# A fused two-block transformer: forget sums packed into spare rows of the first mixer's maps

## The reference, cut to what matters

```python
def forgetting_attention(q, k, v, f_logit):      # 4 heads of 64, 256 tokens
    log_f = jax.nn.log_sigmoid(f_logit)
    c = jnp.cumsum(log_f, axis=1).transpose(0, 2, 1)
    ...
        logits = jnp.einsum("bhqd,bhkd->bhqk", qi, k32) * scale
        logits = logits + ci[..., None] - c[:, :, None, :]
        logits = jnp.where(mask, logits, -jnp.inf)
        probs = jax.nn.softmax(logits, axis=-1)
        return jnp.einsum("bhqk,bhkd->bhqd", probs, v)

def multiscale_pool(v, w_pool, scale):           # 4 groups, causal windows 2, 4, 8, 16
    ...
        mean = (csum - lag) / jnp.minimum(count, w)
        outs.append(mean - g)
```

## Time and profile before

| | before |
|---|---|
| median of the runs | 971.42 us |
| lowest and highest run | 971.24 and 971.78 us |
| span of the profiled execution, first to last instruction | 969.5 us |
| PE busy | 951.9 us (98%) |
| DVE busy | 697.7 us (72%) |
| ACT busy | 521.5 us (54%) |
| POOL busy | 85.5 us (9%) |
| granted TensorE clock, mean over the span | 0.998 |

### The profile page before, as it was taken

The page is one execution under the profiler, slowest core; times in us unless marked ns, Lnnn a source line. Parts: engine busy times, 40 slices in busy tenths (PEclk is TensorE's granted clock), DMA queues, the critical chain, the costliest instruction groups (busy, mean ns, idle before and its releaser), DMA issues.

```text
span 969.5 us, 13640 instructions
## 1 busy us (share of the span) xinstructions
PE 951.9 (98%) x5566; PEld 833.2 (86%) x5566; DVE 697.7 (72%) x922; ACT 521.5 (54%) x707; POOL 85.5 (9%) x110
## 2 busy tenths in 40 slices
PE   9999999999999999999999999999999999999997
PEld 8998888888888798789988888888988798888885
DVE  5889866666658977877676666667989777666663
ACT  5888564444446556865444434368555454443432
POOL 2541100000011100000000000000132110000000
PEclk9999999999999999999999999999999999999999
DMA  9922566556645454145655565557322446756531
GB/s 302 318 94 98 191 222 217 174 182 205 198 153 196 129 165 171 47 131 174 217 174 188 186 192 178 168 172 216 114 88 75 143 143 213 224 184 193 181 122 44
DMA packets 106190, 164.40 MB, mean 170 GB/s; under 512 B 2816, under 2 KB 82784, under 8 KB 106000
## 3 DMA queue, kind: packets, MB, share of 16 engines
q1 hardware_dynamic: 104688, 158.25, 50.8%
q0 software_dynamic: 1440, 5.28, 1.5%
HBM read 162.47 MB, written 1.05 MB: 169 GB/s over the span
## 4 chain that ended last, share of the span: by engine, by line
PE 80%; DVE 12%; ACT 4%; issue 2%; POOL 1%; DMA 0%; SPq 0%; DVEq 0%; ACTq 0%
PE ps L379 78%; DVE wl L1770 3%; PE ps L387 2%; ACT xhl L1195 1%; ACT junk L1177 1%; POOL st L2559 1%; DVE st L2192 1%; DVE xf L1791 1%; DVE xhl L1787 1%; DVE rows L2395 1%; DVE h L1844 1%; DVE hs L1802 1%; DMA prm<-in_prm 0%; ACT SC L1515 0%; DVE hs L2406 0%
## 5 line engine op out<-in xcount | busy, mean ns | idle before, releaser
L1770 DVE TENSOR_TENSOR wl<-raw,wh 128x2048 fp32r<-128x2048 f32 (+2 forms) x146 | 329.8, 2262 | 142.0 <-ACT wh L1189 141.8
L1189 ACT ACTIVATE wh<-raw 128x2048 fp32r<-128x2048 f32 (+2 forms) x150 | 281.8, 1884 | 151.7 <-PE ps L379 144.1
L379 PE MATMUL ps<-xhl,wh 128*128 128x512 f32 (+1 forms) x1248 | 254.7, 350 | 0.3 <-ACT wh L1254 0.3
L379 PEld LDWEIGHTS ps<-xhl,wh 128*128 128x128 f32 x1248 | 199.3, 190 | 27.8 <-issue 1.1
L379 PE MATMUL ps<-wh,xhl 128*128 128x512 f32 (+3 forms) x1000 | 195.5, 339 | 1.6 <-issue 0.9
L379 PEld LDWEIGHTS ps<-wh,xhl 128*128 128x128 f32 x1000 | 155.3, 190 | 20.4 <-issue 1.3
L379 PEld LDWEIGHTS ps<-xhl,wl 128*128 128x128 f32 x1008 | 135.7, 191 | 7.5
L379 PE MATMUL ps<-xhl,wl 128*128 128x256 f32 x1008 | 140.6, 282 | 0.0
L379 PE MATMUL ps<-wl,xhl 128*128 128x512 f32 (+3 forms) x500 | 105.4, 336 | 1.0 <-DVE wl L1770 0.9
L379 PE MATMUL ps<-wh,fh 128*128 128x512 f32 x304 | 91.3, 392 | 1.0 <-DVE fl L2034 0.7
L379 PE MATMUL ps<-wh,fl 128*128 128x512 f32 x304 | 90.4, 390 | 0.0
(11 more groups left out here) (274 smaller groups left out, 840.0 us busy)
## 6 DMA issues: line engine op xcount, KB each, us to landing
raw<-in_ffn_gate SPq DMA_DIRECT2D x22, 1024.0 KB, 5.5
raw<-in_ffn_up SPq DMA_DIRECT2D x22, 1024.0 KB, 5.5
raw<-in_ffn_down SPq DMA_DIRECT2D x22, 1024.0 KB, 4.9
raw<-in_w_up SPq DMA_DIRECT2D x16, 1024.0 KB, 5.6
raw<-in_w_down SPq DMA_DIRECT2D x16, 1024.0 KB, 5.0
raw<-in_s_w_in SPq DMA_DIRECT2D x14, 1024.0 KB, 5.4
raw<-in_w_in SPq DMA_DIRECT2D x9, 1024.0 KB, 9.5
raw<-in_a_w_in SPq DMA_DIRECT2D x6, 1024.0 KB, 5.3
```

The lines of the kernel that those rows point to most:

```text
L379: return e.matmul(o, a, b, start=start, stop=stop, skip_group_check=True)
L1189: e.activation(high_of(i), raw_of(i), ACT.Copy).then_inc(*up("act_high", i))
L1770: e.tensor_tensor(low_of(i), raw_of(i), high_of(i).bitcast(F32), ALU.subtract).then_inc(*up("dve_lo", i))
```

## The change

Three edits, all in the first mixer.

1. The forget logits come from split weights. `wf` is now a compact tile of 8 by 4 columns with one DMA. Two tiles `wfr[0]` and `wfr[1]` of 8 by 128 columns in fp32r are cleared by POOL and then filled at columns 0 to 3 of each group of 32: ACT writes the high part (after the masks), DVE the low part (after the low part of slot 4). PE multiplies them by `xh`, `xl` and `xh`, 24 fp32r matmuls in the place of 8 fp32 ones, and the logits now lie on all four groups of 32 partitions. The softplus runs on 128 partitions.
2. The forget sums ride in the maps' queries and keys. A head has 64 query rows out of 128, the rest were zeros. DVE now writes the sums and ones there (`forget_queries`, `forget_keys`, with 0, 1 and -1 from the table `prm`), and the second fp32 product of each map is gone. `kT` of two tiles becomes `kx` of four, so ACT copies the keys in two instructions. Four memsets of POOL go.
3. The band's second block of tokens covers only the later 128 of the 256 columns.

```diff
-        NCt = sc(256)
-        CQ = sc(256)
-        rk = sc(3, 256)
+        qm = sc(4, 256)
+        kx = sc(4, 256)
+        wfr = [nc.alloc_sbuf_tensor_at(f"wf{i}", [128, 8, 128], F32R, offset=at_s + 4 * (9088 + 1024 * i)) for i in range(2)]
+        wfz = [x[:, :, :].rearrange("p k (g n) -> p k g n", g=4)[:, :, :, 0:4] for x in wfr]
+        wfg = wf.unsqueeze(2).to_broadcast([128, 8, 4, 4])
...
                     mm(o[:, lo:lo + n], q_[:, c], k_[:, 0:n], True, False)
-                    if extra:
-                        mm(o[:, lo:lo + n], extra[0][:, c], extra[1][:, 0:n], False, False)
                     d = mm(o[:, lo + n - 128:lo + n], idb[:, :], mab[:, :], False, True)
...
-                e.wait_ge(*at("dma_wf", 1))
-                for k in range(8):
-                    d = mm(ps[6][0:36, 0:256], wf[:, k, :], xf[:, k, :], k == 0, k == 7)
+                for n, (w, x) in enumerate(((wfr[0], xh), (wfr[0], xl), (wfr[1], xh))):
+                    if n == 0:
+                        e.wait_ge(*at("act_forget_high"))
+                    elif n == 2:
+                        e.wait_ge(*at("dve_forget_low"))
+                    for k in range(8):
+                        d = mm(ps[6][:, 0:256], w[:, k, :], x[:, k, :],
+                               n == 0 and k == 0, n == 2 and k == 7)
...
-                            d = mm(o[:, 256 * i:256 * i + 256], pv[:, tb, 128 * t:128 * t + 128], band[:, 2 * t + i, tb, :],
-                                   tb == 0, tb == 1)
+                            d = mm(o[:, 256 * i + 128 * tb:256 * i + 256], pv[:, tb, 128 * t:128 * t + 128],
+                                   band[:, 2 * t + i, tb, 128 * tb:256], tb == 0, tb == 1)
...
                     e.activation(o[:, :], C(c), ACT.Copy).then_inc(*up("act_masks", i))
+                e.wait_ge(*at("dma_wf"))
+                e.wait_ge(*at("pool_zero", 4))
+                e.activation(wfz[0], wfg, ACT.Copy).then_inc(*up("act_forget_high"))
...
                 lows(4)
+                e.wait_ge(*at("act_forget_high"))
+                e.wait_ge(*at("pool_zero", 4))
+                e.tensor_tensor(wfz[1], wfg, wfz[0].bitcast(F32), ALU.subtract).then_inc(*up("dve_forget_low"))
...
+                def forget_queries(i):
+                    r = slice(64 - 64 * i, 128 - 64 * i)
+                    e.tensor_scalar(qm.rearrange("p (t i) n -> p t i n", i=2)[r, :, i, :],
+                                    ft[r, 1, :].unsqueeze(1).to_broadcast([64, 2, 256]), P("fq", 0)[r], P("fq", 1)[r], ALU.mult,
+                                    ALU.add).then_inc(*up("dve_forget_queries", i))
+                def forget_keys(i):
+                    r = slice(64 - 64 * (i % 2), 128 - 64 * (i % 2))
+                    e.tensor_scalar(kx[r, i, :], ft[r, 1, :], P("fk", 2 * i)[r], P("fk", 2 * i + 1)[r], ALU.mult,
+                                    ALU.add).then_inc(*up("dve_forget_keys", i))
...
-            for i, x in enumerate((wf, wpb, upad, qm, cpad, NCt, CQ)):
+            for i, x in enumerate((cpad, wpb, upad)):
                 e.memset(x, 0.0).then_inc(*up("pool_zero", i))
...
-            e.dma_start(wf[:, :, 0:4], wfv).then_inc(*up("dma_wf", 0))
-            e.dma_start(wf[:, :, 32:36], wfv).then_inc(*up("dma_wf", 1))
+            e.dma_start(wf, wfv).then_inc(*up("dma_wf"))
+            for i, x in enumerate(wfr):
+                e.memset(x[:, :, :].bitcast(F32), 0.0).then_inc(*up("pool_zero", 3 + i))
```

More of the change, by code:

```diff
@@ L33 @@
           ("qn", 3), ("kvn", 2), ("subln", 1), ("s_norm", 4), ("g_norm", 1), ("lb0", 4), ("lb1", 4),
[L34 removed]
+          ("bf", 1), ("dtb", 1), ("alog", 1), ("fq", 2), ("fk", 8), ("eps", 1), ("mhalf", 4)]
 P_AT = {}
@@ L178, in program @@
         sc = Scratch()
-        wf = sc(8, 36)
+        wf = sc(8, 4)
         band = sc(4, 2, 256)
@@ L501, in project_end, with logits @@
                     d.then_inc(*up("pe_sums", n, tb, half))
-            def logits(o, q_, k_, extra=None):
+            def logits(o, q_, k_):
                 for q, (lo, n) in enumerate(((0, 128), (128, 256))):
@@ L611, in first_mixer @@
                 e.wait_ge(*at("act_q", 1))
-                e.wait_ge(*at("act_k"))
+                e.wait_ge(*at("act_k", 1))
                 e.wait_ge(*at("act_masks", 2))
-                e.wait_ge(*at("dve_forget_rows", 3))
+                e.wait_ge(*at("dve_forget_queries", 1))
                 forget_logits(0)
@@ L1273, in taps_and_high @@
                     highs(6)
-                softplus("forget", *(ft[R, i, :] for i in range(4)), junk[R, 0:256], taps_and_high)
-                e.wait_ge(*at("pool_zero", 6))
+                softplus("forget", *(ft[:, i, :] for i in range(4)), junk[:, 0:256], taps_and_high)
                 e.wait_ge(*at("pe_slot", S["q"]))
@@ L1283, in first_mixer @@
                 e.wait_ge(*at("pe_slot", S["k"]))
-                e.activation(kT, ps[0][:, :].rearrange("p (t n) -> p t n", t=2), ACT.Copy).then_inc(*up("act_k"))
+                for i in range(2):
+                    r = slice(64 * i, 64 * i + 64)
+                    e.activation(kx.rearrange("p (t i) n -> p t i n", i=2)[r, :, i, :],
+                                 ps[0][r, :].rearrange("p (t n) -> p t n", t=2), ACT.Copy).then_inc(*up("act_k", i))
                 highs(7)
@@ L1905, in first_mixer @@
                 taps(0, 2)
-                R, F4, G4 = slice(0, 36), slice(0, 4), slice(32, 36)
-                fx, fa, fu, fw = (ft[R, i, :] for i in range(4))
+                fx, fa, fu, fw = (ft[:, i, :] for i in range(4))
                 e.wait_ge(*at("pe_forget"))
-                e.tensor_scalar(fx, ps[6][R, 0:256], P("bf")[R], -1.0, ALU.add, ALU.mult).then_inc(
+                e.tensor_scalar(fx, ps[6][:, 0:256], P("bf"), -1.0, ALU.add, ALU.mult).then_inc(
                     *up("dve_softplus", "forget", "x"))
@@ L1915, in low_and_taps @@
                     taps(6, 9)
-                softplus("forget", fx, fa, fu, fw, junk[R, 0:256], low_and_taps)
+                softplus("forget", fx, fa, fu, fw, junk[:, 0:256], low_and_taps)
                 e.wait_ge(*at("dve_softplus", "forget", "y"))
@@ L1952, in mix_low @@
                         low_part(t0, t0 + 2, tb).then_inc(*up("dve_mix_low", i, tb))
-                for i in range(3):
-                    forget_bias(i)
+                for i in range(2):
+                    forget_queries(i)
+                for i in range(4):
+                    forget_keys(i)
                 lows(7)
@@ L2751 @@
         put(name, src.reshape(k, n // 128, 128).transpose(2, 1, 0).reshape(128, -1))
-    prm[0:4, P_AT["bf"]] = a["b_forget"][0]
-    prm[32:36, P_AT["bf"]] = a["b_forget"][0]
+    for r in range(0, 128, 32):
+        prm[r:r + 4, P_AT["bf"]] = a["b_forget"][0]
     prm[0:8, P_AT["dtb"]] = a["s_dt_bias_2"][0]
     prm[0:8, P_AT["alog"]] = a["s_a_log_2"][0]
-    for i in range(4):
-        prm[i, P_AT["fsel"] + i] = prm[32 + i, P_AT["fsel"] + i] = 1
+    for r in (0, 64):
+        prm[r:r + 4, P_AT["fq"]] = 1
+        prm[r + 32:r + 36, P_AT["fq"] + 1] = 1
+        for i in range(4):
+            prm[r + 32 + i, P_AT["fk"] + 2 * i] = -1
+            prm[r + i, P_AT["fk"] + 2 * i + 1] = 1
     prm[:, P_AT["eps"]] = EPS
```

26 lines of the change are left out of this document (6 added, 20 removed).

## The result

The changed kernel takes 974.13 us (median of 7 runs, 973.92 to 975.12) beside 971.55 for the kernel before on the same chip (7 runs, 971.24 to 971.78): ratio 1.003, 95% interval 1.0021 to 1.0039. It is slower by 2.6 us, where 971.1 was forecast and 974.0 was the top of the range. The profiled execution has a span of 972.2 us, 2.7 more than before.

The account below looks back on a forecast made before the run. PE was taken to bound the kernel, busy 951.9 of 969.5 us. Wait and forget block +3.35, band -0.70, maps -2.84, load -0.15 gave -0.34, so 971.1 us from 971.42; range 969.9 to 974.0.

Parts of the forecast that it names:

- The forget block: Forget logits on PE: 24 fp32r matmuls take 2.88 us where 8 fp32 ones held PE for 3.57.
- the penalty of slot q: Slot q on PE: its 24 matmuls behind the fp32 ones took 0.09 us more than a plain group; this goes.
- the band and the maps: First mixer on PE: halved band matmuls save 0.70 us, dropped fp32 products of four maps save 2.84.
- the load at -0.15: Slot 4's load: one small-piece load fewer lets it land earlier, 0 to -0.6 us, taken as -0.15.
- the clock stands: PE's gap ahead of the forget matmuls: clock stays full, the forecast as summed, 971.1 us; chance 0.59.
- the clock falls: Rival at PE's gap of 4.1 us: clock falls, costing up to 2.9 us, 972.6 to 974.0; chance 0.27.
- 0.9 us of cover stays: Conformer's variance: DVE's square about 0.3 us later, PE 0.2 earlier, so 0.9 us of cover remains and PE does not wait.
- the clock rival: Rival at PE's gap ahead of the forget matmuls: full price of the clock's fall, 2.9 us, gives 974.0; chance 0.18.
- at most at 0.8: Rival at the conformer: cover on DVE or ACT fails, price 0.4 to 0.8 us, 971.9; chance 0.10.

Follow-up runs that it names:

- the gap filled: Changed kernel with 30 fp32r matmuls of discarded result put on PE in the gap ahead of the forget matmuls: 972.38 us, ratio 1.001.
- the early copies: Changed kernel with ACT's forget copy moved behind slot 2's high part and DVE's behind slot 2's low part: 968.27 us, ratio 0.9969.
- the kernel before with the wait: Kernel before the change, its fp32 forget matmuls made to wait for ACT's last mask as well: 977.12 us, ratio 1.0054.
- the moved taps: Kernel of the early copies with ACT's taps 17 and 18 made before its wait for slot h, all work kept: 967.92 us, ratio 0.9965.

## Why the prediction was wrong

**What held.** PE is idle for 3.66 us in front of the forget matmuls, put down to ACT's copy, and starts at 28.30 (28.67 forecast). The copy takes 0.29 us and stands where it was put, behind slot 4 and the masks. DVE's copy costs PE nothing. The forget block takes 2.96 us at full clock (2.88 forecast), the penalty of slot q is gone, and the band and the maps give PE 3.45 us (3.54). Of the 0.37 by which PE started earlier than forecast, 0.28 is slot 4's high part, which began at 25.54 and not at 25.82, where I had put the load at -0.15; but the same part began at 26.19 with the gap filled and at 25.86 with the early copies, where the loads are the same. So I can't say that the load gained anything.

**The first step that failed** is the choice between "the clock stands" (0.59) and "the clock falls" (0.27). All seven runs have a mean clock of 0.994 to 0.997, where the filled gap has 0.998 or 0.999, so it fell in each (0.998 can be either, but none of them has it). In the profiled one it cost 4.45 - 2.88 = 1.57 us, and by the filled gap 1.6. My reason against it was that the fall was seen once, 3.6 us behind the last matmul, and I put the forget block into the sum at 2.88. That was the right doubt, but it cut both ways: here the fall came 4.5 us behind the last matmul, and with the copy ahead of the masks 3.3 behind it. The one fall in the trace should have been read as "about as long as this gap", with a chance well above a half. The price was too high as well: I took the 2.9 us of PE's whole cold start. The half clock lasted from 29.1 to 32.5, 3.4 us, in which half of the work, 1.7 us, is lost. The Trainium skill, page "TensorE: Matmul & The Clock Gate", section "HAM oscillation — how this bites in real kernels", has bursts behind waits of some microseconds start slowly. By that rule, the trace agrees, in most runs and not in all: one of ten runs with the copy ahead of the masks (3.15 us of idle time in the profiled one) and two of five of the kernel before with the wait (4.15 in the profiled one) kept the clock, as far as mean clocks and times tell.

**The second step that failed** is "0.9 us of cover stays". 974.0, the clock rival's number, is met by 0.1 us, but that is luck: 1.6 is the clock, and 1.4 is the loss in the conformer that I had at 0, and at most at 0.8. I had followed DVE from the maps to the square and taken ACT as being in time. But ACT's order behind slot h is fixed: the copy of slot h, slot 9's high part, taps, the band's copies, the exponentials. That order starts when PE ends slot h, ahead of all that the change saves, so it comes 4.5 us later when PE, behind the first two maps, comes 2.4 later. Every microsecond saved on PE between slot h and the conformer is a microsecond less for ACT. Then DVE waits for the exponential (0.57), and POOL, which gets its taps from ACT, has lost its pause ahead of DVE's rounding and slows DVE by 0.58 and 0.54 (2.81 for 2.23 and 2.82 for 2.28): the square is 3.19 us later, not 0.3. It is shown that the loss is made by ACT's order and by POOL beside DVE: with less work for ACT and POOL the lost 1.3 us come back, with less for DVE 0.2 does, since ACT is then next. My account of DVE missed both what comes ahead of it and what runs beside it; the chain lies on DVE itself for some 20 us. In the early copies ACT's lateness is worth 0.3 of the 1.3 us by the moved taps, and the rest is put down to POOL beside DVE by the rows; no run relieved POOL alone. For the 1.43 us of the changed kernel the two were not parted.

**The sum again**, with both steps as measured: 3.76 + 0.88 - 0.10 - 3.45 + 1.43 + 0.2 = 2.7 us, the difference of the spans. Without the gap (early copies) the same change is -3.0 us. What decides its sign is where ACT's copy of 0.29 us stands.

## What to carry to other kernels

When a copy on a second engine is put in front of the engine that bounds the kernel, put it behind the earliest instruction that allows it, since its cost is the whole order ahead of it; here 0.29 us of copy cost 3.8 us of waiting and 1.6 of clock. Price the restart behind a gap by the length of the half clock over two, and where a gap is about as long as a fall that the trace shows, count on the fall. And when work is taken from the bounding engine, follow every other engine from its last wait ahead of the saving, not from the saving: their cover shrinks by what is saved. A saving can also close the pauses of an engine that slows another one.

## What the runs showed of the hardware that was not expected

- The fall is not bound to a fixed distance, and can come once PE is at work again: 4.5 us behind the last matmul and 0.8 into the new work in the changed kernel, 3.3 behind it with the copy ahead of the masks. In the kernel before with the wait it came at 28.75, as PE started (28.72), 4.2 us behind the last matmul. Runs of one kernel differ: 3 of 5 of that kernel fell (4.15 us of idle time in the profiled execution), 7 of 7 of the changed one (3.66), all but one of ten (972.07 us) with the copy ahead of the masks (3.15), as far as mean clocks and times tell.
- 30 matmuls without a reader, 3.76 us of them, held the clock, with 0.50 us of idle time left: the forget block has its full speed, and 11 runs lie between 971.91 and 972.73 us.
- Which of DVE and POOL is slowed goes, in these rows, by which of them was at work first. A DVE subtraction of 128x2048 elements takes 2.28 us when POOL is idle (the one at 42.14 in the changed kernel) and 2.82 when POOL is at an addition as it begins (72.35). When POOL's addition begins inside the subtraction (67.03 in 66.61 to 68.89), the subtraction stays at 2.28 and the addition takes 2.46, where two of them take 1.59 together at 64.62. Three DVE taps take 1.51 us with POOL idle (44.34) and 2.81 beside its additions (69.62).
